# Issuing the loads of x, and half of the last output tile, from ScalarE's queue in a hybrid decoder layer

## The reference

```
ada = silu(c) @ w_ada + b_ada                    # 6 x 1024: shifts, scales, gates
h   = rmsnorm(x, norm_mix_w) * (1 + sc_a) + sh_a
proj = h @ w_in                                  # all projections of both mixers
y_a = gated linear attention (4 heads), y_b = HGRN2 attention (8 heads), chunks of 64 tokens
x   = x + g_a * ((sigmoid(ma) * y_a + sigmoid(mb) * y_b) @ w_out)
h   = rmsnorm(x, norm_ffn_w) * (1 + sc_f) + sh_f
u   = causal depthwise conv of width 3 over (h @ w_up)
x   = x + g_f * ((silu(gate) * up) @ w_down)
out = rmsnorm(x, final_norm_w)
```

## Time and profile before

| | us |
|---|---|
| median of 3 runs | 873.69 |
| lowest and highest of these | 872.52, 874.15 |
| the profiled execution, its own time | 872.45 |
| its span, first to last instruction | 870.7 |
| PE busy | 856.8 |
| DVE busy | 605.6 |
| ACT busy | 487.6 |
| POOL busy | 252.3 |

### The profile page before, as it was taken

How to read it: one execution, slowest core, us unless ns; L and a number is a source line. 1 busy time by engine, 2 the same in 40 slices (tenths; PEclk the granted TensorE clock), 3 DMA queues, 4 the chain that set the end, 5 groups by cost and what they waited for, 6 DMA issues and landing times.

```text
span 870.7 us, 12717 instructions
## 1 busy us (share of the span) xinstructions
PE 856.8 (98%) x4688; PEld 709.6 (81%) x4688; DVE 605.6 (70%) x779; ACT 487.6 (56%) x739; POOL 252.3 (29%) x227
## 2 busy tenths in 40 slices
PE   7999999999999999999999999999999999999996
PEld 6778888887888888888887888888888888888885
DVE  4598988678967867765955466744444444599995
ACT  5576556577558657656756443633333333356574
POOL 2124779624122131230343000211111111534200
PEclk9999999999999999999999999999999999999999
DMA  9996487283544546445226931533333336599902
GB/s 335 357 334 140 105 205 101 70 256 107 170 145 122 149 136 176 118 150 169 81 67 186 156 94 49 146 97 96 96 96 96 96 96 229 115 269 206 240 29 97
DMA packets 149235, 130.21 MB, mean 150 GB/s; under 512 B 4743, under 2 KB 132065, under 8 KB 148928
## 3 DMA queue, kind: packets, MB, share of 16 engines
q1 hardware_dynamic: 136048, 110.84, 42.3%
q0 software_dynamic: 13136, 18.69, 12.7%
HBM read 125.31 MB, written 4.20 MB: 149 GB/s over the span
## 4 chain that ended last, share of the span: by engine, by line
PE 74%; ACT 1%; DVE 1%; issue 0%; ACTq 0%
PE ps L2220 18%; PE ps L2222 17%; PE ps L2221 17%; PE ps L2651 4%; PE ps L2652 4%; PE ps L2653 4%; PE ps L2387 1%; PE ps L2542 1%; PE ps L2543 1%; PE ps L2546 1%; PE ps L2367 1%; PE ps L2389 1%; PE ps L2351 1%; PE ps L2354 1%; PE ps L2399 0%; PE ps L2336 0%
## 5 line engine op out<-in xcount | busy, mean ns | idle before, releaser
L2220 PE MATMUL ps<-h_hi,w_hi 128*128 128x512 f32 (+1 forms) x568 | 223.3, 393 | 0.4 <-DVE w_lo L1852 0.4
L2222 PE MATMUL ps<-h_hi,w_lo 128*128 128x512 f32 (+1 forms) x568 | 219.5, 386 | 0.0
L2221 PE MATMUL ps<-h_lo,w_hi 128*128 128x512 f32 (+1 forms) x568 | 219.4, 386 | 0.0
L2220 PEld LDWEIGHTS ps<-h_hi,w_hi 128*128 128x128 f32 x568 | 106.7, 188 | 23.1 <-issue 1.0
L2221 PEld LDWEIGHTS ps<-h_lo,w_hi 128*128 128x128 f32 x568 | 106.7, 188 | 22.1 <-issue 1.0
L2222 PEld LDWEIGHTS ps<-h_hi,w_lo 128*128 128x128 f32 x568 | 106.7, 188 | 21.7
L983 POOL TENSOR_TENSOR prod<-conv 128x512 f32 x21 | 43.3, 2061 | 219.3 <-DVE conv L2062 219.3
L1384 ACT ACTIVATE conv<-ps,vecs 128x512 f32<-128x512 f32 x42 | 32.5, 777 | 132.3 <-PE ps L2222 123.9
L2058 DVE SCALAR_TENSOR_TENSOR conv<-ps,vecs,conv 128x511 f32<-128x511 f32 x44 | 32.9, 749 | 104.9 <-ACT conv L1384 102.5
L1852 DVE TENSOR_TENSOR w_lo<-raw,w_hi 128x1024 fp32r<-128x1024 f32 x46 | 58.8, 1292 | 56.5 <-ACT w_hi L1025 56.5
L1511 DVE TENSOR_TENSOR w_lo<-raw,w_hi 128x1024 fp32r<-128x1024 f32 x52 | 63.8, 1231 | 2.3 <-ACT w_hi L1017 2.2
(11 more groups left out here) (312 smaller groups left out, 1813.4 us busy)
## 6 DMA issues: line engine op xcount, KB each, us to landing
raw<-in_w_in_dram SPq DMA_DIRECT2D x44, 512.0 KB, 3.9
raw<-in_w_up_dram SPq DMA_DIRECT2D x44, 512.0 KB, 3.8
ada_w<-in_w_ada_dram SPq DMA_DIRECT2D x32, 512.0 KB, 4.5
ada_w<-in_w_ada_dram SPq DMA_DIRECT2D x8, 1024.0 KB, 10.2
g_blocks<-in_w_in_dram SPq DMA_DIRECT2D x24, 256.0 KB, 6.2
hres<-in_w_down_dram POOLq DMA_DIRECT2D x12, 512.0 KB, 9.0
raw<-in_w_down_dram SPq DMA_DIRECT2D x11, 512.0 KB, 5.4
raw<-in_w_out_dram SPq DMA_DIRECT2D x8, 512.0 KB, 5.7
```

Of the source, the lines that this page charges most:

```text
L2220: pe.matmul(dst, a_hi, b_hi, start=start and i == 0, stop=False)
L2221: pe.matmul(dst, a_hi, b_lo, start=False, stop=False)
L2222: last = pe.matmul(dst, a_lo, b_hi, start=False, stop=stop and i == n - 1)
```

## The change

The four loads of x leave SP's list and stand at the head of ScalarE's. The store of the last tile's second-scaled half (columns 0 to 511, the one that ScalarE scales) leaves SP's list too and stands at the end of ScalarE's, with a semaphore of its own. SP then waits for its own four stores and for that one.

```
@@ sync
             ada0_loads(0)
-            for t in range(TT):
-                sp.dma_start(x_tok[:, t], x[0, t * P:(t + 1) * P, :]).then_inc(x_in[t], 16)
             for i in range(PIECES):
@@ sync, end
-            for half, made in ((1, fin_last_dve), (0, fin_last_act)):
-                sp.wait_ge(made, 1)
-                d = slice(half * T, (half + 1) * T)
-                sp.dma_start(out[0, (TT - 1) * P:T, d], prod[:, 2 * (TT - 1) + half]).then_inc(out_done, 16)
-            sp.wait_ge(out_done, 16 * (TT + 1))
+            sp.wait_ge(fin_last_dve, 1)
+            sp.dma_start(out[0, (TT - 1) * P:T, T:2 * T], prod[:, 2 * (TT - 1) + 1]).then_inc(out_done, 16)
+            sp.wait_ge(out_done, 16 * TT)
+            sp.wait_ge(last_out_done, 16)
@@ scalar
+            for t in range(TT):
+                act.dma_start(x_tok[:, t], x[0, t * P:(t + 1) * P, :]).then_inc(x_in[t], 16)
             act.wait_ge(cols_made, 3)
@@ scalar, end
                     act.activation(prod[:, 2 * t], prod[:, 2 * t], ACT.Copy, scale=frs[:, t:t + 1]
                                    ).then_inc(fin_last_act, 1)
+                    act.wait_ge(fin_last_act, 1)
+                    act.dma_start(out[0, t * P:(t + 1) * P, 0:T], prod[:, 2 * t]).then_inc(last_out_done, 16)
```

More of the change, by code:

```diff
@@ L417, in build @@
         out_done = sem("out_done")
+        last_out_done = sem("last_out_done")
         const_made = sem("const_made")
```

## The result

| | us |
|---|---|
| after the change, median of 4 runs | 879.41 (878.46 to 879.63) |
| before, median of 4 runs | 873.84 (872.52 to 874.15) |
| ratio, after to before | 1.007, 95% interval 1.0058 to 1.0081 |
| profiled execution after, its own time and span | 878.46, 876.7 |

The change makes the kernel slower by 0.7%. The forecast was 880.0, in a range of 875.0 to 884.0. Between the two profiled executions the difference is 6.01 us (878.46 less 872.45). The profiled execution after is the fastest of its four; the other three lie 0.95 us and more above it.

The account below looks back on a forecast made before the run. The prediction took PE, its projection start set by w_ada's landing, to bound the kernel. 872.45 + 4.2 (landing) + 3.2 (clock) - 0.1 (store) = 879.75, plus a little scatter: 880.0 us, range 875.0 to 884.0.

Parts of the forecast that it names:

- What bounds the start: Start: projection at 20.39 us hangs on w_ada's first 2 MB landing; any delay there delays the end by as much.
- Part 1: Start: x's loads leave SP, freeing 2.98 us of issue time worth 0; ScalarE's later table load and sigmoid cost 0.
- Part 2: Start: x shares the transfer engines, so w_ada lands at 13.8 instead of 9.6: +4.2 us, bounds +3.4 and +4.9.
- Part 3: Before the first sums: PE idles 5.7 us, its clock falls to half, slowing sums and transposes: +3.2 us, bounds 0 and 7.5.
- The step from the profiled execution to a median: Whole run: median is 1.24 us above the profiled execution; only a small part was added, reaching 880.0 us.
- Part 4: End: ScalarE issues the last half tile's store 0.2 us earlier: -0.1 us, bounds -0.3 and +0.1.
- Late, but warm: Start: w_ada lands at 13.8, but the clock survives or recovers within the sums; 876.6 to 877.8 us, chance 0.20.
- Cold for long: Start: the clock returns only in the projection; 884.2 us, chance 0.10.
- Whole transfers in turn: Start: engines alternate whole transfers, two x pieces pass, w_ada lands at 11.4, clock warm; 874.2 to 875.4 us, chance 0.08.
- Not slower: Start: ScalarE's issues are held back, x stays behind w_ada, PE resumes at 9.6; 872.3 to 873.6 us, chance 0.10.

Follow-up runs that it names:

- the last run: Full change with TensorE's list reordered: transposes of x first, first w_ada sums ahead of the second half of the norm's spread; 871.92 us, ratio 0.9984.
- run 1: Against the full change, the last store is back on SP, only the four loads of x on ScalarE; 879.36 us, ratio 1.0067.
- run 2: Against the full change, the loads of x are back on SP, only the last half tile's store on ScalarE; 872.52 us, ratio 0.9998.

## Why the prediction was right

- **What bounds the start: right.** I held that the chain to the projection hangs on w_ada's landing and that whatever delays the projection delays the end. Measured: 5.79 us at the projection, 6.0 at the end of the span. It holds for a delay; the last run shows that an earlier start is soon held up by the next landing.
- **Part 1, SP's freed issue time worth 0, ScalarE's later table load hidden: right.** c_rep is made at 5.05 (predicted 6.2; the four issues took 2.40 us and not 2.98, and before, ScalarE had stood 0.42 us at this place anyway) and is needed at 14.2.
- **Part 2, w_ada late: right in kind, 0.4 short.** Predicted 13.8 (13.0 to 14.5), measured 14.2. The 0.7 us that I credited for the earlier start of x was 0.3. x landed from 4.6 to 11.3 where I had 4.5 to 9.5: between 4 and 5 us ScalarE's queue moved 20 packets and SP's 327, so the sharing of one for one is not there from the start. That does not matter for w_ada, whose last byte comes when all is through. The 384 GB/s that I read "in each microsecond from 4 on" is 378 to 423 up to 14 us and 326 right behind that the earlier trace rows; only the 0.7 us rested on it.
- **Part 3, the clock: right in kind, too large.** It fell in the gap, as forecast. The term of 3.2 us measured 1.23 in the profiled execution and 2.1 in that of run 1 (1.69 in the sums, 0.43 behind them); with the fillers, the median moved by 2.1 too. The mis-sized step is that the sums would run at half clock throughout and the turns for a good part (1.95, and 1.25 behind): the clock came back before the sums had ended, or 0.9 us behind (18.9 against 17.98 in run 1).
- **The step from the profiled execution to a median: right for a reason that I only guessed.** I added a small part of the 1.24 us between them. Most runs of before fall in two groups because of the same clock, and after the change it is low in every run: 0.994 or 0.995 on the mean in all nine of the full change and run 1, 0.998 in the four with 36 fillers.
- **Part 4, the store: right within its bounds.** -0.1 predicted, nothing seen, run 2 at 0.9998.
- **Sum.** 4.2 + 3.2 - 0.1 stands against 4.58 + 1.23 and 0.2 elsewhere: +7.3 against +6.0 between the profiled executions, and against 4.6 + 2.1 and some 0.3 in a usual run. The median of 879.41 lies 6.96 above the 872.45 from which I counted. It came within 0.6 of 880.0 because the two errors, 1.1 too much for the clock and 0.4 too little for the landing, have opposite signs; that is luck.
- **The rivals.** "Late, but warm" is what the run with 36 fillers makes, 877.3 where I had 876.6 to 877.8; the change itself was never there. "Cold for long" did not occur. "Whole transfers in turn" is refuted by the first piece of w_ada, which landed behind all of x. That rival also called a gap of 3.3 us "warm", since it is shorter than the tail's 4.3: the runs have the clock down behind gaps of 2.0 to 2.4 us, so the tail's one fall did not allow that. "Not slower" needed x to wait behind w_ada, and its first packets went ahead.

## What to carry to other kernels

Two transfers that are issued in one queue keep their order; issued from two queues they share the same full engines, one row for one row once both are under way, so the one with the longer rows wins and the other lands when both are done. Before moving a load to another queue, ask what it then passes, and who waits for that. Here the move stops costing only when the engine that uses the loads is reordered to take first what now lands first, and then it gains 0.16% at best.

## What the runs showed of the hardware

- Two hardware queues with rows under way are served one row for one, whatever the size: 231 rows beside 231 (x's of 4 KB against 1 KB), 432 beside 433, and 1282 beside 1302 at equal size. The start times of the single rows alternate (0.04 and 0.16 us apart). It is not so in the first microseconds: 20 beside 327 in the kernel after, from 4 to 5 us.
- A transfer issued beside another queue's backlog can start late: x's first row moved 3.8 us after its issue with SP's queue full, 1.0 us with it empty; w_ada's first row moved 2.4 us after its issue beside x, 1.1 us alone.
- The clock can be down after a gap of 2.0 to 2.4 us between two stretches of work (2.3, 2.4 and 1.97 in three executions, with the sums at 3.5 to 3.6 us in place of 1.95). Over many executions of one program this makes two groups of time, 872.1 to 872.8 and 873.7 to 874.6, with some runs between them; filler work in the gap removes the upper group.
